# Pooling means as shifted additions on VectorE over turned input, in place of band-matrix products on TensorE

## What is computed

```python
POOL_WINDOWS = (2, 4, 8, 16); POOL_GROUP = 128
def pool_mixer(p, pool_w, pool_b, pool_scale):      # p: 256 tokens x 512
    cs = jnp.cumsum(pf, axis=1)
    for g, w in enumerate(POOL_WINDOWS):
        c = cs[..., sl]                             # the 128 columns of group g
        prev = jnp.pad(c, ((0, 0), (w, 0), (0, 0)))[:, :s]
        cnt = jnp.minimum(t + 1, w)
        outs.append((c - prev) / cnt - pf[..., sl]) # trailing mean of w tokens, minus the token
    y = jnp.einsum('bsgc,gcd->bsgd', pooled, pool_w) + pool_b
    return y.reshape(b, s, POOL_WIDTH) * pool_scale
```

## Time and profile before

| what | value |
|---|---|
| median of 3 runs | 2047.79 us (2047.72 to 2047.92) |
| profiled execution | 2047.9 us, its span 2046.1 us |
| TensorE busy | 2035.9 us (100% of the span) |
| VectorE busy | 1388.8 us (68%) |
| ScalarE busy | 1019.8 us (50%) |
| GpSimd busy | 93.8 us (5%) |
| mean granted TensorE clock | 0.999 of full |

### The profile page before, as it was taken

How to read it: one execution, slowest core, us unless ns; L and a number is a source line. 1 busy time by engine, 2 the same in 40 slices (tenths; PEclk the granted TensorE clock), 3 DMA queues, 4 the chain that set the end, 5 groups by cost and what they waited for, 6 DMA issues and landing times.

```text
span 2046.1 us, 25163 instructions
## 1 busy us (share of the span) xinstructions
PE 2035.9 (100%) x10372; PEld 1719.1 (84%) x10372; DVE 1388.8 (68%) x1620; ACT 1019.8 (50%) x1286; POOL 93.8 (5%) x133
## 2 busy tenths in 40 slices
PE   9999999999999999999999999999999999999998
PEld 7888888888888888888888888888888888888887
DVE  5555686775757666777575667757767677577675
ACT  6444586454444345775443365644534466444331
POOL 1001010000010001100100000000100000000000
PEclk9999999999999999999999999999999999999999
DMA  8655444465556555544656474555755645455552
GB/s 317 212 196 170 170 165 144 151 210 196 193 182 225 185 177 194 172 144 144 215 194 193 158 246 148 173 165 171 245 187 188 202 156 190 160 185 189 197 191 82
DMA packets 225938, 377.73 MB, mean 185 GB/s; under 512 B 6577, under 2 KB 113201, under 8 KB 225825
## 3 DMA queue, kind: packets, MB, share of 16 engines
q1 hardware_dynamic: 221840, 362.64, 53.2%
q0 software_dynamic: 3984, 13.49, 2.2%
HBM read 375.05 MB, written 1.05 MB: 184 GB/s over the span
## 4 chain that ended last, share of the span: by engine, by line
PE 97%; DVE 2%; DMA 0%; ACT 0%; issue 0%; DVEq 0%; POOL 0%; ACTq 0%; POOLq 0%
PE pb L1629 63%; PE pb L1640 18%; PE pb L1643 9%; PE pb L1652 2%; PE pb L1698 1%; DVE wl L2077 1%; PE pb L1776 1%; DMA raw<-in_ffn_w_up_dram 0%; PE pb L1775 0%; PE pb L1657 0%; PE pb L1763 0%; PE pb L1833 0%; PE pb L1755 0%; DVE lS L2260 0%; PE pb L1783 0%; PE pb L1691 0%
## 5 line engine op out<-in xcount | busy, mean ns | idle before, releaser
L1859 ACT ACTIVATE wh<-raw 128x2048 fp32r<-128x2048 f32 (+4 forms) x351 | 658.4, 1876 | 620.7 <-PE pb L1629 251.7
L2077 DVE TENSOR_TENSOR wl<-raw,wh 128x2048 fp32r<-128x2048 f32 (+4 forms) x351 | 782.4, 2235 | 160.8 <-ACT wh L1859 160.3
L1629 PE MATMUL pb<-wh,x 128*128 128x512 f32 (+2 forms) x2160 | 656.3, 386 | 0.0
L1629 PEld LDWEIGHTS pb<-wh,x 128*128 128x128 f32 x2160 | 403.6, 188 | 78.6
L1629 PE MATMUL pb<-wl,x 128*128 128x512 f32 (+2 forms) x1080 | 424.5, 393 | 2.2 <-DVE wl L2077 2.2
L1640 PE MATMUL pb<-x,wh 128*128 128x512 f32 x1568 | 397.0, 395 | 0.0
L1640 PEld LDWEIGHTS pb<-x,wh 128*128 128x128 f32 x1568 | 283.3, 189 | 51.9
L1629 PE MATMUL pb<-wl,mh 128*128 128x512 f32 (+1 forms) x740 | 255.7, 391 | 0.0
L1629 PE MATMUL pb<-wh,ml 128*128 128x512 f32 (+1 forms) x740 | 253.7, 388 | 0.0
L1629 PE MATMUL pb<-wh,mh 128*128 128x512 f32 (+1 forms) x740 | 253.4, 388 | 0.0
L1629 PEld LDWEIGHTS pb<-wl,x 128*128 128x128 f32 x1080 | 202.9, 188 | 45.4 <-DVE wl L2077 3.8
(11 more groups left out here) (362 smaller groups left out, 1591.2 us busy)
## 6 DMA issues: line engine op xcount, KB each, us to landing
raw<-in_w_in_dram SPq DMA_DIRECT2D x100, 1024.0 KB, 5.2
raw<-in_w_ff_dram SPq DMA_DIRECT2D x64, 1024.0 KB, 5.4
raw<-in_ffn_w_down_dram SPq DMA_DIRECT2D x44, 1024.0 KB, 5.0
raw<-in_ffn_w_up_dram SPq DMA_DIRECT2D x43, 1024.0 KB, 5.2
raw<-in_ffn_w_gate_dram SPq DMA_DIRECT2D x42, 1024.0 KB, 5.2
raw<-in_w_branch_dram SPq DMA_DIRECT2D x24, 1024.0 KB, 5.0
raw<-in_w_out_dram SPq DMA_DIRECT2D x16, 1024.0 KB, 5.0
raw<-in_w_in_dram SPq DMA_DIRECT2D x4, 832.0 KB, 4.2
```

The costliest lines, as they stand in the source:

```text
L1629: ins = e.matmul(pb[b][:, 0:c1 - c0], x[:, s, cols], w[:, n, c0:c1], start=(it["first"] and n == 0 and q == 0), stop=(it["stop"] and n == ...
L1859: e.activation(hi, raw, ACT.Copy).then_inc(m.high_done, 1)
L2077: e.tensor_tensor(lo, raw, hi.bitcast(F32), ALU.subtract).then_inc(m.low_done, 1)
```

## The change

Both halves of `pin` are turned by TensorE (`pinturn`, four transposes each, after wide 2 and wide 3 in the planner's steps) and copied by ScalarE to `pp`, a tile with 16 zero columns ahead of each group's 256 tokens. VectorE forms the sums of 2, 4, 8 and 16 tokens by shifted additions, in two items (`sums` 0 and 1), corrects the first 16 tokens, and a third item (`pooling`) scales and subtracts the token. `poolmix`, `poolbias` and `poolsplit` are the same work, later in the list. The band matrix, its two loads and its products are gone; one small constant, `c_short`, is loaded once in `consts`.

```diff
         def pool():
+            uses = []
+            for t in range(2):
+                yield
+                uses.append(self.side())
+                v = self.pe("pinturn", t=t, use=uses[t], need=[pin[t]])
+                self.add("pincopy", t=t, use=uses[t], p=v["p"])
+            self.pin_free = [v["p"]]
+            for i in range(2):
+                yield
+                self.add("sums", i=i, need=[("evac", u) for u in uses])
+            yield
+            self.add("pooling", n=l)
             yield
             yield
             for i in range(2):
                 use = self.side()
-                v = self.pe("poolsum", i=i, use=use, need=list(pin), l=l)
-                self.add("poolcopy", i=i, use=use, p=v["p"])
-                got = use
-                yield
-            self.pin_free = [v["p"]]
-            for i in range(2):
-                use = self.side()
-                v = self.pe("poolmix", i=i, use=use, need=[("evac", got)], l=l)
+                v = self.pe("poolmix", i=i, use=use, need=[("pooled", l + 1)], l=l)
                 self.add("poolbias", i=i, use=use, p=v["p"], l=l)
                 yield
             self.add("poolsplit", use=use, n=l)
...
+            e.dma_start(m.short[:, :, :], m.A["c_short"].partition_broadcast(P)).then_inc(m.short_landed, 16)
...
-            e.dma_start(m.pc[:, :], m.A["c_pool"]).then_inc(m.pc_landed, 16)
...
+        elif k == "pinturn":
+            bank = pb[use[0]]
+            pe.all_ready(it["need"])
+            pe.wait_ge(m.evac[use[0]], use[1])
+            for c in range(4):
+                ins = e.transpose(bank[:, c * P:c * P + P], m.pin[:, t, c * P:c * P + P], ident[:, :])
...
-            for g in (2 * i, 2 * i + 1):
-                o, gs = (g % 2) * S, slice(g * P, g * P + P)
-                e.matmul(bank[:, o:o + 256], m.pin[:, 0, gs], m.pc[:, 256 * g:256 * g + 256], start=True, stop=False,
-                         skip_group_check=True)
-                ins = e.matmul(bank[:, o + 128:o + 256], m.pin[:, 1, gs], m.pc[:, 1024 + P * g:1024 + P * g + P],
-                               start=False, stop=True, skip_group_check=True)
...
-        elif k == "poolcopy":
+        elif k == "pincopy":
             a.pe(p)
-            e.activation(m.pair_of(("pT", i)), bank[:, :], ACT.Copy).then_inc(m.evac[use[0]], 1)
+            e.activation(m.pT[:, :, t * P:t * P + P], bank[:, :].rearrange("p (g n) -> p g n", n=P),
+                         ACT.Copy).then_inc(m.evac[use[0]], 1)
...
+        elif k == "sums":
+            pp, sa, sb, end = m.pp, m.sa, m.sb, 16 + S
+            v.all_ready(it["need"])
+            if i == 0:
+                v.step(e.memset(pp[:, :, 0:16], 0.0))
+                v.own_steps()
+                v.step(e.tensor_tensor(sa[:, :, 1:end], pp[:, :, 1:end], pp[:, :, 0:end - 1], ALU.add))
+                v.own_steps()
+                v.step(e.tensor_tensor(sb[:, :, 3:end], sa[:, 1:4, 3:end], sa[:, 1:4, 1:end - 2], ALU.add))
+            else:
+                v.own_steps()
+                v.step(e.tensor_tensor(sa[:, 2:4, 7:end], sb[:, 1:3, 7:end], sb[:, 1:3, 3:end - 4], ALU.add))
+                v.own_steps()
+                v.step(e.tensor_tensor(sb[:, 2, 15:end], sa[:, 3, 15:end], sa[:, 3, 7:end - 8], ALU.add))
+                v.own_steps()
+                v.wait_ge(m.short_landed, 16)
+                sums = m.window_sums()
+                for g in range(4):
+                    v.step(e.tensor_tensor(sums[g][:, 0:16], sums[g][:, 0:16], m.short[:, g, :], ALU.mult))
+        elif k == "pooling":
+            v.own_steps()
+            for g, x in enumerate(m.window_sums()):
+                ins = e.scalar_tensor_tensor(m.pT[:, g, :], x, 0.5 ** (g + 1), m.pT[:, g, :], ALU.mult,
+                                             ALU.subtract)
+            ins.then_inc(m.pooled, 1)
```

More of the change, by code:

```diff
@@ L45, in constants @@
     freq = np.broadcast_to(np.stack([f1, f1, f2, f2]).reshape(1, 64), (P, 64))
[L46 to L54, removed]
+    short = np.array([[w / min(t + 1, w) for t in range(16)] for w in (2, 4, 8, 16)], np.float32)
     s = q[:, None]
@@ L61, in constants @@
         "c_ident": ident, "c_mask": mask, "c_freq": np.ascontiguousarray(freq),
-        "c_pool": np.ascontiguousarray(np.concatenate([p0, p1], 1)),
+        "c_short": short,
         "c_tril": np.concatenate([tril, chunk], 1),
@@ L99, in __init__ @@
         self.gq_landed, self.sub_landed = s("gq_landed"), s("sub_landed")
-        self.pc_landed, self.pw_landed = s("pc_landed"), s("pw_landed")
+        self.short_landed, self.pw_landed, self.pooled = s("short_landed"), s("pw_landed"), s("pooled")
         self.c_squared, self.kr_copied, self.c_rstd = s("c_squared"), s("kr_copied"), s("c_rstd")
@@ L122, in __init__ @@
         self.out_landed = s("out_landed")
-        self.event = {"pe": self.pe_done, "split_low": self.split_low, "pool_low": self.pool_low, "normed": self.normed,
+        self.event = {"pe": self.pe_done, "split_low": self.split_low, "pool_low": self.pool_low, "pooled": self.pooled, "normed": self.normed,
                       "h_scaled": self.h_scaled, "combined": self.combined, "exp_done": self.exp_done,
@@ L182, in sbuf @@
         self.bn = A("bn", take(128), [P, 2, 16])
+        self.short = A("short", take(256), [P, 4, 16])
         self.epsc = A("epsc", take(32), [P, 8])
@@ L235, in sbuf @@
         self.kT = A("kT", o_kt, [P, 8, S])
-        self.pc = A("pc", o_kt, [P, 1536])
-        self.pw = A("pw", o_kt + 6144, [P, 4, P])
+        self.pw = A("pw", o_g[1] + 4352, [P, 4, P])
+        self.pp = A("pp", o_g[1], [P, 4, 16 + S])
+        self.pT = self.pp[:, :, 16:16 + S]
+        self.sa = A("sa", o_m + 16384, [P, 4, 16 + S])
+        self.sb = A("sb", o_m + 16384 + 4352, [P, 3, 16 + S])
         self.rope_tmp = A("rope_tmp", o_xn, [P, 512])
@@ L240, in sbuf @@
         self.cl = A("cl", o_xn + 3072, [P, 3, S], F32R)
-        self.pT = A("pT", o_g[1], [P, 4, S])
         o_gq = rt(1536)
@@ L336, in half, with window_sums @@
         return self.cols[name][:, 2 * q + i, :]
+    def window_sums(self):
+        return [x[:, g, 16:16 + S] for x, g in ((self.sa, 0), (self.sb, 0), (self.sa, 2), (self.sb, 2))]
     def row(self, name, t):
@@ L1080, in mixer1 @@
             self.pump()
-        pool_done = []
         def pool():
+            uses = []
[10 more added lines that the diff above has]
+            self.add("pooling", n=l)
             yield
@@ L1102, in pool @@
             self.g_free[1] = ("pool_low", l + 1)
-            self.kt_free = v["p"]
-            pool_done.append(True)
         self.lanes[3].append(pool())
@@ L1118, in mixer1 @@
         self.group(self.cols(W, l, 1440, 0, self.copy_t("dv", self.dv)))
-        while not pool_done or ("C", 2, 1) not in self.ready or ("C", 2, 0) not in self.ready:
+        while ("C", 2, 1) not in self.ready or ("C", 2, 0) not in self.ready:
             self.pump()
@@ L1645, in pe_program @@
             ins.then_inc(m.pe_done, 1)
+        elif k == "pinturn":
[4 more added lines that the diff above has]
+                ins = e.transpose(bank[:, c * P:c * P + P], m.pin[:, t, c * P:c * P + P], ident[:, :])
+            ins.then_inc(m.pe_done, 1)
         elif k == "turn":
@@ L1919, in act_program @@
             e.activation(m.row(it["dst"], t), bank[:, :], ACT.Copy).then_inc(m.evac[use[0]], 1)
-        elif k == "poolsum":
-            pass
-        elif k == "poolcopy":
+        elif k == "pincopy":
             a.pe(p)
-            e.activation(m.pair_of(("pT", i)), bank[:, :], ACT.Copy).then_inc(m.evac[use[0]], 1)
+            e.activation(m.pT[:, :, t * P:t * P + P], bank[:, :].rearrange("p (g n) -> p g n", n=P),
+                         ACT.Copy).then_inc(m.evac[use[0]], 1)
         elif k == "poolsplit":
             a.emptied(use)
-            e.activation(m.yph[:, :, :].rearrange("p a s -> p (a s)"), m.pT[:, :, :].rearrange("p a s -> p (a s)"),
-                         ACT.Copy).then_inc(m.pool_high, 1)
+            e.activation(m.yph[:, :, :], m.pT[:, :, :], ACT.Copy).then_inc(m.pool_high, 1)
         elif k == "qsave":
@@ L2240, in dve_program @@
         elif k == "poolsplit":
-            pT, hi, lo = [w[:, :, :].rearrange("p a s -> p (a s)") for w in (m.pT, m.yph, m.ypl)]
             v.wait_ge(m.pool_high, n + 1)
-            e.tensor_tensor(lo, pT, hi.bitcast(F32), ALU.subtract).then_inc(m.pool_low, 1)
+            e.tensor_tensor(m.ypl[:, :, :], m.pT[:, :, :], m.yph[:, :, :].bitcast(F32), ALU.subtract).then_inc(m.pool_low, 1)
         elif k == "krrope":
```

## The result

| | us |
|---|---|
| before, median of 17 executions | 2047.79 (2047.41 to 2048.39) |
| changed, median of 17 executions | 2050.74 (2048.95 to 2053.83) |
| ratio | 1.0018, 95% interval 1.0011 to 1.0024 |
| profiled execution of the changed kernel | 2049.34, its span 2047.6 |

By the medians the changed kernel is 2.95 us slower, 0.14%. The ratio in the table is taken over all executions, and its interval lies wholly above 1. More telling than the median is the spread: executions of the kernel before lie within 1 us of each other, those of the changed kernel within 5, at about 2049.0, 2050.5, 2052.1 and 2053.7, and the mean granted clock that goes with them falls from 0.999 to 0.997. The profiled execution is one of the shortest, so its trace shows what the change does at full clock.

What follows compares the result with a forecast made beforehand. TensorE was taken as the bound, 97% of the chain of waits. 2 x (-1.74 us of TensorE work + 2.39 of new idle time) = +1.3 us on 2047.9, median 0.1 lower: 2049.1 us, range 2044.3 to 2053.5.

Steps and rivals of the forecast that it cites:

- TensorE's work: Per layer, two poolsums (2.61 us) go and two turns of four transposes (0.87) come: 1.74 us less.
- the tail: Second poolmix, second bias and poolsplit, now behind tokens 2 and 3; bias, high and low part add 3.25 us after the softmax.
- Order of the list: Yields counted against ticks: second poolmix after tokens 2, poolsplit after tokens 3; score products end 2.60 us earlier.
- VectorE before the scores: New pooling work of 5.8 us per layer before the scores stays hidden, 1.7 us cover; rival that it comes late: 8%.
- The full chain: Softmax to second head's product: 3.25 us added, begun 2.60 earlier, so product 0.65 us later; TensorE idle some 2.6 per layer.
- the wait for the bank of dv: Second query product may wait half a microsecond for its bank, inside the same 2.6 us of idle time.
- The clock: TensorE's granted clock after the new idle time before the second head's product; no loss from it in the forecast sum.
- The rival: Idle time over 2 us drops the clock to 1.2 GHz until the next pair's scores, up to 6 us per layer: 2061; 4%.
- the row of 1.68 us: Profile row of the kernel before: TensorE's longest idle time, 1.68 us, in a stretch showing full clock, 1.00.
- a doubled pooling chain: Rival before the scores: pooling costs twice its 5.8 us, exceeding the cover by 4.1 us per layer: 2057.3 us.
- The sign of being wrong: One of three listed signs in the changed profile: the clock in this stretch is under 1.00.
- The side: Chances by 0.2% margin: faster 0.03, within 0.86, slower 0.11.

Runs made afterwards that it cites:

- the tail ahead of the scores: Changed kernel with both poolmix, both biases and poolsplit together behind wide 8, before the scores; 2044.32 us, ratio 0.9983 to the kernel before.
- the band products with the late tail: Kernel before, only second poolmix, second bias and poolsplit moved behind tokens 2 and 3; 2055.80 us, again 2056.36 us (ratios 1.0037, 1.0043).

## Why the prediction was right or wrong

**TensorE's work**: right. It is 1.74 us less per layer, as the earlier trace rows priced it: the tail ahead of the scores gets back 3.4 us of the 3.5.

**Order of the list**: right. The softmax began 2.51 us earlier (2.60 forecast; the whole execution was 0.09 late at this place), the tail stood where the count of yields had put it.

**VectorE before the scores**: right in kind, 5.8 us was too much. From start to start the pooling instructions take 2.39 + 1.54 + 1.34 = 5.3 us, because the small ones start 0.09 us apart and the scalings 0.33 (0.10 and 0.40 taken). The cover of the pooling work (the time between its end and the product that needs it) was 2.3 us where the forecast's times give 1.9; that of the first bias, which ends at 242.57 while the scores start at 244.29, was the forecast's 1.7. The Trainium skill's formula (VectorE: DVE Perf Modes, section on the TRN2 errata) fits each addition (1.29 us at 1084 elements) and the corrections (0.17 at 16), but not the MEMSET (0.11 us, where an estimate by it is 0.22), and adding it up, 6.0 us, overstates a row of independent instructions.

**The full chain**: right. Addition 3.26 us (from 255.03 to 258.29) for 3.25; product at 262.75 for 262.65; idle time 2.2 + 0.3 for 2.6, the 0.3 being the wait for the bank of dv that was foreseen. At full clock the result is 2049.3 and the forecast was 2049.1. One slip of the working: its own idle time of 2.6 us puts TensorE's readiness at 260.1 us, not 259.9, and the sum doesn't use it.

**The clock**: here the prediction failed, in a term taken as nothing. The rival had the place and the mechanism right and was given 4%; in fact, by their times, the clock fell in 23 of 28 executions, in one layer or in both. The step that failed is the inference from the row of 1.68 us at full clock to 2.2 us. That row is a single execution at the start of the program, and no row of before had 2 us of idle time within dense work, so nothing spoke for a low chance. What the runs showed instead: at this place 1.24 us kept the clock, and 2.2 us lost it in most executions. The price of a fall was overstated: up to 6 us per layer was the bound, 1.6 and 3.0 were measured, so the two medians lie 1.6 and 2.9 us above the 2049.1 of the chain alone. That they stay inside the range is in part luck, because its upper end, 2053.5, was set by a doubled pooling chain (half of whose excess gives 2053.2, a small slip) and not by the clock, and single executions went beyond it, up to 2055.31. The sign of being wrong that the forecast named, a clock under 1.00 in this stretch, came true. The rule of the Trainium skill that an idle TensorE falls back to half its clock (TensorE: Matmul & The Clock Gate, Part 1) is borne out by the rows at 0.50.

**The side**: 86% was given to a change within 0.2%. The measured one is within it, 0.14% by the medians and 0.18% by the ratio, whose interval reaches to 0.24%. That it is slower at all follows from the tail, and half of the median's 2.95 us is the clock's.

## What to carry to other kernels

When work is moved off the bound engine, ask first what stands behind its new place in the other engines' queues: here a free-looking tail of 3.25 us was put between two links of a chain that had no slack, and one yield less per poolmix turned +4.3 us into -3.4 on the same chip. Where TensorE comes to stand idle in one piece, its cost isn't only the idle time: compare the spread and the mean clock of many executions, not one trace, and if the wait cannot be removed, useless products in it can pay: here they made the median 2.6 us shorter.

## What was not expected of the hardware

- The granted clock fell to 0.50 behind a single idle time of 2.2 us in the midst of dense work, in 23 of 28 executions by their times, and stayed at full behind 1.24 us (11 of 11) and, in the one trace that has it, behind 1.68 us at the start of the program. It fell as TensorE took up work again in one layer and over a microsecond later in the other. It is a matter of the single execution: one binary gave 2048.8 and 2055.3 us on one chip.
- Behind the same 2.2 us the time at the low clock differed: it cost 3.0 us in layer 0 and 1.5 in layer 1 of one and the same execution, that of the band products with the late tail. What decides between the two, and whether it falls at all, was not tested.
